# Transposing the attention probabilities by VectorE blocks and a trip through memory instead of TensorE transposes, in a hybrid pool, attention and convolution layer

## What is computed

```python
h = rms_norm(x, norm_g) * (1 + scale) + shift
proj = h @ w_in                  # 2048 x 13824, split among the branches and their gates
# sliding-window attention: 16 query heads, 4 key heads, head size 64, a sink logit per head
s = einsum('bnqhgd,bnkhd->bnhgqk', qc, kb) * HEAD_DIM ** -0.5, masked by chunks of 64
m = maximum(max(s), sink)
p = exp(s - m); p = p / (sum(p) + exp(sink - m))
o = einsum('bnhgqk,bnkhd->bnqhgd', p, vb)
y_attn = o * silu(attn_z)
merged = g_pool * (y_pool @ w_branch_pool) + g_attn * (y_attn @ w_branch_attn) + g_conv * (y_conv @ w_branch_conv)
out = rms_norm(x + gate * (merged @ w_out), final_g)
```

## Time and profile before

| what | value |
|---|---|
| device time, median of 3 runs | 934.45 us (933.88 to 934.46) |
| time of the profiled execution | 934.39 us |
| its span, first to last instruction | 932.5 us |
| mean granted TensorE clock | 0.998 |
| busy share of the span: PE, DVE, ACT, POOL | 97%, 76%, 44%, 5% |
| DMA traffic | 228.43 MB, mean 245 GB/s |

### The profile page before, as it was taken

How to read it: one execution, slowest core, us unless ns; L and a number is a source line. 1 busy time by engine, 2 the same in 40 slices (tenths; PEclk the granted TensorE clock), 3 DMA queues, 4 the chain that set the end, 5 groups by cost and what they waited for, 6 DMA issues and landing times.

```text
span 932.5 us, 10230 instructions
## 1 busy us (share of the span) xinstructions
PE 903.5 (97%) x4147; PEld 726.3 (78%) x4147; DVE 712.6 (76%) x810; ACT 413.2 (44%) x380; POOL 47.8 (5%) x78
## 2 busy tenths in 40 slices
PE   1999999999999999999999999999999999999996
PEld 1668677888888888888877778888888888888885
DVE  4778796888978767777789886685677988866783
ACT  3446252634244344434554665357434443344332
POOL 2000000135100000011011000000000000000000
PEclk9999999999999999999999999999999999999999
DMA  9999999999746566578666547657779998965512
GB/s 334 387 386 387 385 340 371 331 260 255 219 159 208 181 189 208 190 215 239 203 196 191 175 136 162 205 170 156 254 266 393 377 315 292 348 211 186 181 46 91
DMA packets 114160, 228.43 MB, mean 245 GB/s; under 512 B 7762, under 2 KB 7842, under 8 KB 113345
## 3 DMA queue, kind: packets, MB, share of 16 engines
q1 hardware_dynamic: 106768, 213.15, 68.3%
q0 software_dynamic: 7056, 13.84, 5.3%
q10 hardware_dynamic: 288, 0.79, 0.2%
HBM read 221.43 MB, written 6.29 MB: 244 GB/s over the span
## 4 chain that ended last, share of the span: by engine, by line
PE 92%; DMA 3%; DVE 3%; issue 1%; ACT 1%; SPq 0%; DVEq 0%; ACTq 0%
PE acc_odd L1312 13%; PE acc_odd L1314 13%; PE acc_odd L1313 13%; PE acc_even L1312 12%; PE acc_even L1314 12%; PE acc_even L1313 12%; PE side_a L1312 2%; PE side_a L1314 2%; PE side_a L1313 2%; PE side_b L1372 2%; DMA raw<-in_w_ada 1%; DMA x_tok<-in_x 1%; DVE gate_sums L1133 1%; PE side_b L1312 1%; PE side_b L1314 1%
## 5 line engine op out<-in xcount | busy, mean ns | idle before, releaser
L794 DVE TENSOR_TENSOR wl<-raw,wh 128x2048 fp32r<-128x2048 f32 x147 | 335.8, 2288 | 136.5 <-ACT wh L511 136.0
L511 ACT ACTIVATE wh<-raw 128x2048 fp32r<-128x2048 f32 x147 | 280.6, 1914 | 283.7 <-PE acc_odd L1314 117.8
L1312 PE MATMUL acc_even<-wh,act_h 128*128 128x512 f32 x430 | 169.5, 394 | 0.0
L1312 PE MATMUL acc_odd<-wh,act_h 128*128 128x512 f32 x432 | 169.3, 392 | 0.0
L1313 PE MATMUL acc_odd<-wl,act_h 128*128 128x512 f32 x432 | 168.2, 389 | 0.0
L1314 PE MATMUL acc_odd<-wh,act_l 128*128 128x512 f32 x432 | 168.1, 389 | 0.0
L1314 PE MATMUL acc_even<-wh,act_l 128*128 128x512 f32 x430 | 167.5, 389 | 0.0
L1313 PE MATMUL acc_even<-wl,act_h 128*128 128x512 f32 x430 | 167.5, 389 | 0.0
L1017 DVE SCALAR_TENSOR_TENSOR conv_slots<-conv_slots,taps 128x256 f32<-128x256 f32 x240 | 100.1, 478 | 0.2
L1312 PEld LDWEIGHTS acc_even<-wh,act_h 128*128 128x128 f32 x430 | 80.7, 188 | 19.6 <-issue 2.5
L1312 PEld LDWEIGHTS acc_odd<-wh,act_h 128*128 128x128 f32 x432 | 81.1, 188 | 19.1 <-issue 2.2
(11 more groups left out here) (288 smaller groups left out, 951.1 us busy)
## 6 DMA issues: line engine op xcount, KB each, us to landing
raw<-in_w_in SPq DMA_DIRECT2D x106, 1024.0 KB, 5.9
raw<-in_w_ada SPq DMA_DIRECT2D x48, 1024.0 KB, 9.3
raw<-in_w_out SPq DMA_DIRECT2D x16, 1024.0 KB, 5.0
raw<-in_w_branch_pool SPq DMA_DIRECT2D x8, 1024.0 KB, 5.0
raw<-in_w_branch_attn SPq DMA_DIRECT2D x16, 512.0 KB, 6.7
raw<-in_w_branch_conv SPq DMA_DIRECT2D x8, 1024.0 KB, 6.0
raw<-in_conv_pw SPq DMA_DIRECT2D x4, 1024.0 KB, 5.6
x_tok<-in_x SPq DMA_DIRECT2D x2, 1024.0 KB, 9.4
```

The lines of the kernel that those rows point to most:

```text
L511: nc.scalar.activation(wh[:, m % RING], raw[SLOT_OF[g]][:, :, :], ACT.Copy).then_inc(high_done, 1)
L794: nc.vector.tensor_tensor(wl[:, m % RING], raw[SLOT_OF[load_of(m)]][:, :, :], wh[:, m % RING].bitcast(F32), ALU.subtract).then_inc(raw_don ...
L1312: nc.tensor.matmul(sums, xh, wh[:, slot, i, :], start=begin, stop=False)
```

## The change

It takes the transposes of the probabilities off PE and the copies off ACT. After `normalize(u)` DVE transposes the probabilities in blocks of 32x32 into `probs_blocks`, one instruction of 128x512 for an even unit and two for an odd one. POOL stores them with four DMAs to a scratch tensor (`store_probs`, among the stores and loads of `q1` and `z1`), and ACT's queue loads them back turned with one DMA (`load_probs`, 256 KB or 512 KB) four steps after the scores. `unit_values` and `attend` move from three to five steps after the scores, and all units start one step earlier (`score_step` is 70 + 2u). The scratch is read as `j b n a i -> b j (n a i)`, as the queries are. `probs_t` becomes two buffers, for even and odd units. Since buffers are shared, three operations of ACT get a wait for a store of odd probabilities: `za1` in step 75, `ga0` in step 79, `zc0` in step 87; the block transposes of units 1 and 3 wait for the loads of `q0` and `q1`. Taps move ahead: five in each of the steps 27 to 69, two in the steps 70 to 85, one in step 86. `turn_blocks` of `q0` and `q1` moves one step earlier, that of `z1` one step later.

```diff
-TAPS_AT = {m: 4 for m in range(27, 89)}
+TAPS_AT = {m: 5 if m < 70 else 2 for m in range(27, 87)}
+TAPS_AT[86] = 1
...
-            return 71 + 2 * u
+            return 70 + 2 * u
...
+            def store_probs(u):
+                pool.wait_ge(probs_blocked, u + 1)
+                for a_ in range(4):
+                    pool.dma_start(probs_scratch[u].rearrange("j b n a i -> j (b n) a i")[:, :, a_, :],
+                                   blocks_of(u)[QUAD * a_:QUAD * (a_ + 1), :, :, :].rearrange("j b n i -> j (b n) i")
+                                   ).then_inc(probs_stored[u % 2], 16)
+            store_probs(0)
             store_blocks("q1")
             load_turned("q1", q_chan[:, 1, :, :])
+            for u in range(1, 4):
+                store_probs(u)
             store_blocks("z1")
             load_turned("z1", zs_attn[:, 4:8, :])
+            for u in range(4, UNITS):
+                store_probs(u)
...
-            def copy_probs(u):
...
+            def load_probs(u):
+                act.wait_ge(probs_stored[u % 2], 64 * (u // 2 + 1))
+                if u >= 2:
+                    act.wait_ge(pv_done, u - 1)
+                act.dma_start(probs_t[u % 2][:, :, :].rearrange("p k c -> p (k c)"),
+                              probs_scratch[u].rearrange("j b n a i -> b j (n a i)")).then_inc(probs_loaded[u % 2], 16)
...
                 if m == 75:
-                    act.wait_ge(blocks_ready, TURNS.index("z0") + 1)
+                    act.wait_ge(turned["q0"], 16)
+                    act.wait_ge(probs_stored[1], 64)
                     take_heads("za1", z_tok, ACT.Silu)
                 for u in range(UNITS):
-                    if m == score_step(u) + 2:
-                        copy_probs(u)
+                    if m == score_step(u) + 4:
+                        load_probs(u)
...
+                dve.wait_ge(probs_ready, u + 1)
+                if u >= 2:
+                    dve.wait_ge(probs_stored[u % 2], 64 * (u // 2))
+                if u in (1, 3):
+                    dve.wait_ge(turned["q0" if u == 1 else "q1"], 16)
+                for kt in range(u % 2 + 1):
+                    dst = blocks_of(u)[:, :, GROUP * kt:GROUP * (kt + 1), :].rearrange("p b g i -> p g b i")
+                    last = nc.vector.transpose(dst, heads[:, :, P * kt:P * (kt + 1)].rearrange("p g (b j) -> p g b j", b=4))
+                last.then_inc(probs_blocked, 1)
...
-            def unit_transpose(u):
...
             def unit_values(u):
                 h = u % 2
-                pe.wait_ge(probs_copied, u + 1)
+                pe.wait_ge(probs_loaded[h], 16 * (u // 2 + 1))
...
-                    if m == score_step(u) + 3:
+                    if m == score_step(u) + 5:
                         unit_values(u)
```

More of the change, by code:

```diff
@@ L177, in program @@
     probs = at("probs", [P, GROUP * SEQ], F32, 152 * KB)
-    probs_t = at("probs_t", [P, 2, COLS], F32, 156 * KB)
+    probs_t = [at("probs_t0", [P, 1, COLS], F32, 201 * KB + 2944), at("probs_t1", [P, 2, COLS], F32, 156 * KB)]
     zs_attn = at("zs_attn", [P, BT, SEQ], F32, 176 * KB)
@@ L185, in program @@
     blocks = {name: at(f"blocks_{name}", [P, 4, 4, TH, QUAD], F32, offset * KB)
-              for name, offset in (("glu0", 176), ("u0", 180), ("u1", 184), ("glu1", 196), ("z0", 184), ("q0", 184), ("q1", 184), ("z1", 188))}
+              for name, offset in (("glu0", 176), ("u0", 180), ("u1", 184), ("glu1", 196), ("z0", 184), ("q0", 192), ("q1", 184), ("z1", 188))}
+    probs_blocks = [at("probs_blocks0", [P, 4, GROUP, QUAD], F32, 142 * KB)] + [
+        at(f"probs_blocks{n}", [P, 4, 2 * GROUP, QUAD], F32, offset * KB) for n, offset in ((1, 192), (3, 184))]
+    probs_scratch = [nc.dram_tensor(f"probs_turned_{u}", (QUAD, 4, GROUP * (u % 2 + 1), 4, QUAD), F32,
+                                    kind="Internal").ap() for u in range(2 * KV_HEADS)]
     scratch = {name: nc.dram_tensor(f"turned_{name}", (QUAD, 4, 4 * TH, 4, QUAD), F32, kind="Internal").ap()
@@ L292, in program @@
         exp_done, probs_ready = sem("exp_done"), sem("probs_ready")
[L293 removed]
+        probs_blocked = sem("probs_blocked")
+        probs_stored = [sem("probs_even_stored"), sem("probs_odd_stored")]
+        probs_loaded = [sem("probs_even_loaded"), sem("probs_odd_loaded")]
         pv_done, attn_ready = sem("pv_done"), sem("attn_ready")
@@ L369, in score_step, with blocks_of @@
         def score_step(u):
-            return 71 + 2 * u
+            return 70 + 2 * u
+        def blocks_of(u):
+            return probs_blocks[0 if u % 2 == 0 else 2 if u == 3 else 1]
         @block.sync
@@ L720, in _ @@
                         act.wait_ge(turned[("q1", "z1")[j]], 16)
+                    if j == 0:
+                        act.wait_ge(probs_stored[1], 64 * 2)
                     gate_sigmoid(f"ga{j}", j % 2, 3 + j)
@@ L1063, in score_max @@
                 dve.wait_ge(scores_done, u + 1)
-                if u:
-                    dve.wait_ge(probs_td, u)
-                else:
+                if u == 0:
                     dve.wait_ge(sink_loaded, 16)
@@ L1097, in attention_low @@
                 dve.wait_ge(y_high, 3 + p)
-                dve.wait_ge(probs_td, UNITS)
+                dve.wait_ge(pv_done, UNITS if p else 1)
                 nc.vector.tensor_tensor(y_l[:, tiles, :], zs_attn[:, tiles, :], y_h[:, tiles, :].bitcast(F32), ALU.subtract
@@ L1194, in _ @@
                     turn_blocks("z0", z_tok[:, :, :])
-                if m == 65:
+                if m == 64:
                     dve.wait_ge(*freed("q0"))
+                    turn_blocks("q0", q_tok[:, :, :])
+                if m == 72:
+                    dve.wait_ge(*freed("q1"))
                     dve.wait_ge(turned["z0"], 16)
[L1198 to L1201, removed]
                     turn_blocks("q1", q_tok[:, :, :])
-                if m == 77:
+                if m == 78:
                     dve.wait_ge(*freed("za1"))
@@ L1497, in unit_scores, with unit_values @@
                 ins.then_inc(scores_done, 1)
-            def unit_transpose(u):
+            def unit_values(u):
                 h = u % 2
-                width = P * (h + 1)
-                pe.wait_ge(probs_ready, u + 1)
+                pe.wait_ge(probs_loaded[h], 16 * (u // 2 + 1))
                 if u:
                     pe.wait_ge(attn_ready, u)
[L1505 to L1513, removed]
-                pe.wait_ge(probs_copied, u + 1)
+                else:
+                    pe.wait_ge(k_copied, 1)
                 for kt in range(h + 1):
@@ L1519, in unit_values @@
                                                kv_tok[:, kt, first:first + HEAD_DIM],
-                                               probs_t[:, kt, PAIRS * P * j:PAIRS * P * (j + 1)],
+                                               probs_t[h][:, kt, PAIRS * P * j:PAIRS * P * (j + 1)],
                                                start=(kt == 0), stop=(kt == h), tile_position=(0, HEAD_DIM * j))
```

9 lines of the change are left out of this document (2 added, 7 removed).

## The result

| what | before | changed |
|---|---|---|
| device time, median (range) | 934.26 us (933.88 to 934.46), 4 runs | 953.6 us (952.2 to 958.18), 4 runs |
| time and span of the profiled execution | 934.39, 932.5 us | 958.18, 956.0 us |
| mean granted TensorE clock | 0.998 | 0.985 |
| busy share of PE, DVE, ACT, POOL | 97%, 76%, 44%, 5% | 95%, 75%, 43%, 7% |

The ratio is 1.0216 (95% interval 1.0203 to 1.0229): 19.3 us slower. The forecast was 943.6, with 952 as its upper end. The profiled execution is the longest of the four (the spans of the others are 950.1 to 951.9 us), so what the trace shows is some 5 us more than a typical execution; no trace shows one of the others.

What follows compares the result with a forecast made beforehand. PE was taken to bound the kernel, busy 97% and never waiting after the first weights. From 934.4 us, 5.3 saved and 14.5 of new waits (net +9.2) gave 943.6, with an 8-in-10 range of 930.5 to 952.

Steps and rivals of the forecast that it cites:

- the time of a load beside the weights: Loads of the probabilities: 5.5 us even, 8.6 odd alone; 1.2 added beside weights, 6.7 and 9.8; upper bounds 7.7 and 12.9.
- Saved on PE: Attention units: 48 transposes taken off PE, eight worth 0.89 us and four 0.45, in all 5.3 us saved.
- DVE and ACT at no cost: Block transposes (8 us on DVE), fifth taps (0.4 us a step) and ACT's DMA issues are hidden, costed at nothing.
- rival 4: DVE becomes the bound in five-tap or attention steps and PE waits for `wl`: about 948 us, chance 0.05.
- Loads on four engines: ACT's loads of the probabilities are split over four of 16 DMA engines only, at 84 GB/s, by their four-fold slowest dimension.
- rival 1: ACT's queue spreads the load over all 16 engines, only unit 1 waits: 929.6 to 933.0 us, chance 0.20.
- Unit 1: PE before values 1: load issued at 35.7 us, landed at 45.5, wanted at 37.4; wait 8.1 us, the largest term.
- unit 3: PE before values 3: 8.6 us left for a load of 9.8, a wait of 1.2 us.
- unit 7: PE before values 7: 6.5 us left for a load of 9.8, a wait of 3.3 us.
- Units 0 and 5: PE before values 0 and 5: waits for the loads of 0.7 and 1.2 us.
- rival 3: A PE wait of 8 us lets the granted clock fall, a piece takes 5.5 us more: 949 us, chance 0.12.
- The store behind the `q1` load: POOL's queue: unit 1's store lands at 28.5 us if held by the `q1` load, 25.1 if not; 28.5 taken.

Runs made afterwards that it cites:

- The ceiling run: Changed kernel without stores and loads of the probabilities; the values multiply the resident `kv_tok` and wait for DVE's blocks only: 928.79 us, ratio 0.9938.
- the first two experiments: Changed kernel with each load of the probabilities as four DMAs, first one for each `b` (943.75 us), then split by columns (963.39 us).
- each part by rows: Changed kernel, each load of the probabilities cut into four DMAs, one for each `b`, with 32 rows as slowest dimension: 943.75 us.
- each by columns: Changed kernel, each load of the probabilities cut into four DMAs, each with all four `b` as slowest dimension: 963.39 us.
- all three edits: Changed kernel with four-DMA loads by `b` for the probabilities and for `q1` and `z1`, and a place of its own for unit 1's blocks: 928.92 us.
- The edits on that load alone: Changed kernel with only POOL's loads of `q1` and `z1` split into four DMAs by `b`: 953.23 us.
- on the order: Changed kernel with the probabilities' loads as four DMAs by `b` and unit 1's store ahead of the load of `q1` on POOL's queue: 940.86 us.
- freeing ACT alone: Changed kernel with a place of its own for unit 1's blocks, so that `za1` needn't wait for their store: 960.38 us.
- Experiment 12: The 928.9 us kernel (four-DMA loads throughout, own place for unit 1's blocks) with each load of the probabilities again one DMA: 948.73 us.

## Why the prediction was wrong

The sign, the mechanism and the three longest waits were placed right, the size was not: +19.3 us (+23.8 in the profiled execution) where the sum said +9.2. Two steps failed: the time of a load beside the weights, and the clock, which the sum put at nothing. The profiled execution is 14.6 us over the forecast: 8.9 of waits, with nearly 2 of slow values in them, 4.9 of other work at the lower clock, 1.1 of waits for `raw`, less 0.3 saved on PE.

- **Saved on PE:** 5.3 forecast. The ceiling run is 5.6 under the kernel before of its own chip (934.43 less 928.79). In the traces the eight and four transposes are gone, and scores alone take 0.73 (even) and 1.15 (odd) beyond the spacing, as the earlier trace rows gave and as estimated from the earlier trace rows. Right.
- **DVE and ACT at no cost:** right, by the same run; rival 4 falls with it.
- **Loads on four engines:** right, by the first two experiments; rival 1 falls. The rule of the Trainium skill ("DMA: Bandwidth & Descriptors", section "Why a DMA increments its semaphore by 16 and not by 1"), that both kinds of queue take the largest number of engines up to 16 that divides the slowest dimension of both patterns, would give each part by rows 16 engines and each by columns four. The traces agree: 0.79 of the engines against 0.27, and 943.75 against 963.39 us.
- **Unit 1:** 8.1 forecast, 9.2 measured. From the end of piece 71 (458.7): the load of `q1` issued at +16.9 (forecast 16.3) and landed at +31.3 or later (28.5); the store issued at +19.7 (19.0), landed at +33.9 (28.5); load 1 issued at +37.7 (35.7), landed at +46.1 (45.5). The store landed 5.4 later than forecast. Two terms made up for it: ACT's sequencer issues the load before the engine has done the exponentials and the split, so only 3.8 us follow the store's landing and not 7.2, and the load itself took 8.4 and not 9.8. The term was right partly by luck.
- **The load's time beside the weights** is the step that failed: "they themselves take 1.2 more in the median than at the least, and I add as much". The 1.2 us are a median over the whole span, while the earlier trace rows also have a landing of 16.9; the weight loads issued beside load 3 took 14.7 us in the median themselves. A load on four engines took 8.4 us with the weights stopped, but 15.4 at unit 3 and 20.5 at unit 7, beyond the upper bound of 12.9. So unit 3 waited 3.0 and not 1.2, unit 7 9.2 and not 3.3. Load 7 was even issued 0.3 us after the end of piece 87 and not 5.2, or the wait would have been longer by as much. Units 0 and 5 had no wait (0.7 and 1.2 forecast): their loads, too, went out earlier than the engine's order had suggested. Load 7's 20.5 us have two parts. From 577 to 583 no packet of its queue moved, while the weights' queue (q1) had the engines full; from 583 to 597 its 0.52 MB went, beside the weights (packets, MB, share):

```profile
q1 hardware_dynamic: 632, 1.20, 96.0%
q10 hardware_dynamic: 132, 0.52, 16.7%
```

The first part isn't the four engines: with all three edits load 7 also moved nothing for 4.5 us or more after its issue at 559.5 (2 packets up to 565), and then 0.50 MB in the 3 us from 565 to 568, where four engines took 14. Why it is held wasn't tried. A window from the time in which the load is issued but not moving:

```profile
578.00:582.00 4.00, 4.00 (x19) 3.28 (x19) 0.30 (x1) 3.67 (x3) 0.00 (x0) 1.00 1.05 219
```

- **The clock** was kept apart as rival 3, with its own chance, though the forecast itself held a wait of 8.1 us, longer than the 3.5 us after which the earlier trace rows show the first fall. The rival's condition was thus met by the forecast, and its price belonged in the sum. It cost about 5 us behind three waits, even that of 3.0 us; the rival had 5.5 for one. Forecast and rival 3 together are 949, still 4.5 under the median.
- **The store behind the `q1` load:** the choice of 28.5 over 25.1 was the right one, and still short. The edits on that load alone (10.0 in place of 14.1 us for ACT) and on the order (9.0) show the holding. What the Trainium skill says ("DMA: Bandwidth & Descriptors", section "Queues, rings and completion order"), that each DMA engine consumes descriptors in ring order, stands there for the hardware queues of SP and ACT. If it holds for POOL's software queue too, a store can start on these four engines only behind the load; the trace agrees as far as these 4 to 5 us go. The other 9 us of ACT's stop are the store's own issue and landing, for which the forecast took 6.1 from `q1`'s store.

## What to carry to other kernels

A DMA whose slowest dimension is four runs on four engines; cut it along that dimension into parts with more rows there (here 32). Its time beside a saturating stream can't be had from the median of the stream's own transfers: here 512 KB took 8.4 us with the stream stopped and 11.7 to 20.7 beside it, where each of the four parts by rows took 1.9 to 8.8. Where the sum holds a long wait of TensorE, it must hold the clock that the wait costs. Where a wait of one engine is mended, ask what it had been holding back: freeing ACT alone cost 6.8 us in the medians, most likely since the weights then run beside the slow load, while with fast loads the same edit brought 9.4.

## What the runs showed of the hardware

- ACT's sequencer issued DMAs while the engine still had earlier instructions to do (496.37, with the exponentials of unit 2 running until 497.9 and the split before the DMA until 499.8), by 3.4 us there and 4.8 us at unit 7 (576.90, the split ending at 581.7). A term that adds up the engine's work before a DMA's issue is too long.
- After PE stopped at 495.6 the granted clock held 1.00 until 500 and needed until about 511 to come back, though PE was at work again from 504.8. At unit 3 PE stopped at 533.7 for 3.0 us, and the clock fell at 538.
- In the window 578 to 582 all 16 DMA engines are busy (share 1.05) at 219 GB/s, about half of the 412 of the earlier trace rows, while `w_branch_attn` (loads of 512 KB) is under way. Load 7, issued at 576.90, moves no packet before 583. Why these loads are slow, and why load 7 is held, wasn't tried.
- Most kernels in which PE waits for loads scatter (952.2 to 958.2, 936.4 to 943.1), those in which it doesn't have 0.6 us between the shortest and longest (928.87 to 929.47). Experiment 12, with 15.1 us of waits, has only 0.9 (947.96 to 948.89).
